# Six PSUM banks in place of two for the blocks of the FFN's input projection

## What is computed

```
def conv_ffn(h, w_in, conv_w, conv_b, w_out):
    u = dwconv_centred(jnp.einsum('bsd,df->bsf', h, w_in), conv_w, conv_b)
    gate, up = jnp.split(u, 2, axis=-1)
    return jnp.einsum('bsf,fd->bsd', jax.nn.gelu(gate, approximate=True) * up, w_out)
```

## Time and profile before

| what | before |
|---|---|
| median of three runs | 1570.83 us (1568.6 to 1573.79) |
| the profiled execution | 1573.15 us, span 1571.3 us |
| TensorE matmul busy | 1429.5 us, 91% |
| VectorE busy | 781.9 us, 50% |
| GpSimd busy | 690.0 us, 44% |
| ScalarE busy | 638.2 us, 41% |
| granted TensorE clock, mean | 0.952 of full |

### The profile page before, as it was taken

One profiled execution on the slowest core, in us unless ns is written; L12 is line 12 of the kernel. 1 busy time (PEld: TensorE's weight loads), 2 busy tenths in 40 slices (PEclk: granted clock), 3 DMA queues, 4 the chain that ended last, 5 costly groups with the idle time before them and its releaser, 6 DMA issues.

```text
span 1571.3 us, 15335 instructions
## 1 busy us (share of the span) xinstructions
PE 1429.5 (91%) x6054; PEld 1107.1 (70%) x6054; DVE 781.9 (50%) x936; ACT 638.2 (41%) x934; POOL 690.0 (44%) x339
## 2 busy tenths in 40 slices
PE   6899798989969999999997699987959999999994
PEld 4678565777846777777886477876737777778883
DVE  5435596661046766676001645355066676673004
ACT  5443474543334344434222455534334434443221
POOL 5343584023553444434554443422653444435543
PEclk9999899999988999999999699998969999999998
DMA  4222000012312332232332132310212332223331
GB/s 175 76 82 90 24 1 17 31 41 67 94 54 67 94 92 86 92 94 87 99 88 88 51 87 87 92 43 1 81 41 81 94 94 91 86 93 90 94 98 53
DMA packets 34631, 117.67 MB, mean 75 GB/s; under 512 B 3840, under 2 KB 4224, under 8 KB 34560
## 3 DMA queue, kind: packets, MB, share of 16 engines
q1 hardware_dynamic: 33840, 114.63, 23.5%
q10 hardware_dynamic: 720, 2.06, 0.4%
HBM read 114.58 MB, written 2.10 MB: 74 GB/s over the span
## 4 chain that ended last, share of the span: by engine, by line
PE 44%; DVE 29%; ACT 12%; issue 3%; DMA 0%; DVEq 0%; ACTq 0%
PE bank L254 12%; PE bank L257 12%; PE bank L258 12%; DVE cbuf L458 10%; ACT cbuf L502 4%; DVE cbuf L462 4%; ACT whi L230 3%; DVE ubuf L467 2%; DVE cbuf L532 2%; DVE cbuf L364 2%; DVE xw_lo L354 2%; ACT g_hi L511 2%; ACT cbuf L508 2%; PE bank L986 2%; DVE xres L374 1%
## 5 line engine op out<-in xcount | busy, mean ns | idle before, releaser
L238 POOL TENSOR_TENSOR wlo<-raw,whi 128x1024 fp32r<-128x1024 f32 (+2 forms) x217 | 505.3, 2331 | 752.1 <-ACT whi L230 752.1
L254 PE MATMUL bank<-xw_hi,whi 128*128 128x512 f32 x1224 | 509.1, 416 | 76.7 <-DVE xw_lo L354 62.9
L257 PE MATMUL bank<-xw_lo,whi 128*128 128x512 f32 x1224 | 492.2, 402 | 0.0
L258 PE MATMUL bank<-xw_hi,wlo 128*128 128x512 f32 x1224 | 492.1, 402 | 0.0
L254 PEld LDWEIGHTS bank<-xw_hi,whi 128*128 128x128 f32 x1224 | 234.7, 192 | 170.9 <-issue 54.6
L230 ACT ACTIVATE whi<-raw 128x1024 fp32r<-128x1024 f32 (+2 forms) x217 | 221.0, 1022 | 248.2 <-DMA raw<-in_fout 131.9
L258 PEld LDWEIGHTS bank<-xw_hi,wlo 128*128 128x128 f32 x1224 | 235.0, 192 | 57.3
L257 PEld LDWEIGHTS bank<-xw_lo,whi 128*128 128x128 f32 x1224 | 235.8, 193 | 56.0 <-issue 3.9
L458 DVE SCALAR_TENSOR_TENSOR cbuf<-ubuf,par,cbuf 128x510 f32<-128x510 f32 x100 | 183.4, 1834 | 126.5 <-ACT cbuf L502 115.9
L347 DVE RECIPROCAL rstd<-ubuf 128x512 f32<-128x512 f32 x4 | 13.4, 3353 | 363.8 <-ACT ubuf L324 363.8
L254 PE MATMUL bank<-g_hi,whi 128*128 128x512 f32 x352 | 139.4, 396 | 0.0
(11 more groups left out here) (240 smaller groups left out, 1486.0 us busy)
## 6 DMA issues: line engine op xcount, KB each, us to landing
raw<-in_fin SPq DMA_DIRECT2D x88, 512.0 KB, 3.5
raw<-in_fout SPq DMA_DIRECT2D x32, 448.0 KB, 3.2
raw<-in_gin SPq DMA_DIRECT2D x25, 512.0 KB, 3.6
raw<-in_hin SPq DMA_DIRECT2D x24, 512.0 KB, 3.5
raw<-in_hout SPq DMA_DIRECT2D x16, 512.0 KB, 3.5
raw<-in_fout SPq DMA_DIRECT2D x16, 512.0 KB, 3.5
raw<-in_gout SPq DMA_DIRECT2D x8, 512.0 KB, 3.5
xres<-in_x SPq DMA_DIRECT2D x8, 256.0 KB, 6.3
```

Of the source, the lines that this page charges most:

```text
L238: nc.gpsimd.tensor_tensor(wlo[s][:, 0:n], raw[s][:, 0:n], whi[s][:, 0:n].bitcast(F32), ALU.subtract).then_inc(w_lo, 1)
L254: first = nc.tensor.matmul(out_ap, wh, ah, start=start and k == 0, stop=False)
L257: nc.tensor.matmul(out_ap, wh, al, start=False, stop=False)
L258: last = nc.tensor.matmul(out_ap, wl, ah, start=False, stop=stop and k == kts - 1)
```

## The change

```diff
@@ -280,6 +280,8 @@
                     c = 2 * t + u
                     if c >= 2:
                         pe.wait_ge(sem("out_m"), of("out_m", k) + c - 1)
+                    elif k in (1, 3):
+                        pe.wait_ge(sem("fin_u"), of("fin_u", k // 2) + 2 * FF - 1 + c)
                     for b in range(per):
                         src_hi, src_lo, k0, ready = a_of_block(b)
                         if ready is not None and c == 0:
@@ -470,7 +472,7 @@
 
 
         def fbank(ft, u):
-            return bank[u if ft == 0 else 2 + u]
+            return bank[(2 * ft + u) % 6]
 
         def pe_fin(pe, l):
             base = BASE[f"fin{l}"]
@@ -478,8 +480,8 @@
 
             def body(t, ft):
                 for u in range(2):
-                    if ft >= 2:
-                        pe.wait_ge(sem("fin_u"), of("fin_u", l) + 2 * t - 1 + u)
+                    if ft >= 3:
+                        pe.wait_ge(sem("fin_u"), of("fin_u", l) + 2 * t - 5 + u)
                     if ft == 0 and u == 1:
                         product_and_res(pe, r, base + 1, fbank(ft, u)[:])
                     else:
```

## The result

The changed kernel takes 1573.85 us (median of 20 runs, 1571.25 to 1577.66) against 1571.16 us before (20 runs, 1568.01 to 1574.78). The ratio of the runs is 1.0021, with a 95% interval of 1.0011 to 1.0030, that is 1.7 to 4.7 us (the medians by themselves differ by 2.7 us). The interval leaves out 1.0, so the changed kernel is slower, by an amount that is small beside the spread of 6 us between its own runs.

A forecast was written before the change was run, and what follows sets the result against it. Fin was taken as bound by a ring of VectorE and ScalarE, 11.57 us a turn. Late fout starts (0.56 us) plus half clock (3.2) gave 3.8 us more, median 1570.83 to 1574.6 us, range 1570 to 1578.5.

The forecast's parts named there:

- No gain in fin: In fin, removing bank waits gains 0 on the path, since VectorE and ScalarE keep their 11.57 us turn.
- The next hold: In fin from block 17 on, TensorE waits for `w_lo` in place of the bank, about 14 times a layer.
- The late first matmul: At the handover, fout's first matmul starts 0.35 us late, net 0.28 us a layer, 0.56 in all.
- The ring's change: In fin, the ring of VectorE and ScalarE does not move and keeps its 11.57 us a turn.
- The clock: At the handover, TensorE's 3.75 us pause drops the clock, costing 1.6 us a layer, 3.2 in all, ends 0 and 4.4.
- Rival A: In fin, the bank holds the path, so the change gains 17.6 us in all: 1553.2 us; chance 0.05.
- Rival B: At the handover, no clock fall in one or both pauses, or shorter pause: 0.6 to 2.2 us lost; chance 0.20.
- rival C: Behind the handover pauses, half clock lasts 4.5 us or more each: for example 1575.8 or 1577.5 us; chance 0.25.
- Rival D: Inside fin, the clock falls too, at the pause each turn on `w_lo`: 33 us, 1604 us; chance 0.02.

The follow-up runs named there:

- e4: Kernel before (two banks), with ScalarE making the weights' high part of block j+3 behind the centre tap of block j: ratio 0.9912 to before.
- e1: Changed kernel (six banks), but TensorE waits until block j-2 has been taken out, so it can't run ahead: ratio 0.9999 to before.
- e2: Changed kernel with eight extra matmuls, results never read, between fin's last block and fout's first wait in both layers: ratio 1.0009 to before.
- e6: Changed kernel, but block 43 waits until block 41 has been taken out, which splits the pause: ratio 1.0015 to before.
- e3: Kernel before with four banks for fin (2 to 5), fout's chunks in banks 0 and 1 as before: ratio 1.0011 to before.
- e5: Changed kernel (six banks), with ScalarE making the weights' high part of block j+3 behind the centre tap of block j: ratio 0.9901 to before.

## Why the prediction was right

The forecast was 3.8 us more; the stages show 4.15, the runs 3.3 (1.7 to 4.7). Its mechanism is confirmed step by step; of its sizes one term that it put at nothing was not nothing, and that the half clock lasted as chosen was in part luck.

- No gain in fin: right. The ring kept its turn of 11.57 to 11.58 us. e4 shows directly that it was the ring, not TensorE, that set the turn.
- The next hold is the weights' low part, from block 17 on: right in place (block 17 starts behind a pause at 568.68, which is 82.93 us after the first block is taken out; the prediction's own numbers give 501.70 + 6 x 11.57 = 571.12, which is 82.8 behind 488.36). The waits do not name it, they say "issue"; the timeline does.
- The late first matmul: 0.28 us a layer net was forecast, 0.25 of it as a later start (in fin) and 0.10 of restart less 0.07 given back (in fout). Both are right: from block 42's `ubuf` instruction to fout's first matmul it is 0.74 us in place of 0.48 or 0.49, and fout is 0.03 to 0.05 us longer where the clock stays up in it (e1, e2, e6).
- The ring's change was put at nothing, and here the sum was short. From the first block taken out to block 42 it is 242.11 and 242.21 us in place of 241.95 and 241.89, so 0.16 and 0.32 us more. The first taps of the gate blocks (u=0) take 0.25 and 0.20 us more over the 22 turns. With six banks but no running ahead (e1) the same stretch is 241.94 and 241.90 us; in e2, e3 and e6, which all run ahead, it is 242.09 to 242.20. So the ring is slightly sensitive to when TensorE and the loads work, contrary to the prediction. Why the taps grew was not tried.
- The clock: 1.6 us a layer was chosen, from the pause of 3.05 us rather than that of 4.45 us. It was 3.4 us at half clock in both layers, and e2 prices it at 1.56 and 1.54 us. That the choice by the nearer length came out is partly luck, since the length of the pause does not set it: the very pause of 4.45 us brought 6.8 us of half clock, part of it inside the pause, in six of the eight kernels' profiled executions and 3.4 us in the two others (e1 and e5), and the pause of 1.98 us in e6 brought 3.4 us as well.
- Rival A (a gain) is out by the chain and by e3. Rival B (the clock stays up) and rival C (4.5 us of half clock or more) did not happen in the profiled execution; in other executions either may have, and the runs' times do not show it. Rival D (the clock falls in fin) did not happen: the window of 500 to 700 us reads 1.00.

A reader of the runs alone would have little to go by: the spans of the two profiled executions differ by only 1.6 us, since the changed kernel's came to fin 2.6 us earlier (485.75 against 488.36). No instruction ahead of that point differs between the two, and over the eight profiled executions it lies anywhere from 483.03 to 488.36 us (the last section shows one reason).

## What to carry to other kernels

Before giving an engine more buffers, follow the chain through the repeated wait. If it closes on the other engines, the buffers only let this engine run ahead to the next shared limit, and the time that it used to lose in small pieces can come back as one long pause where the stages meet. For TensorE one long pause can cost more than many short ones, because the clock can fall behind it. Shorten the ring first (here one instruction moved behind another, 13.6 us); after that it mattered little here whether there were two banks or six.

## What the runs showed of the hardware

- A pause of 1.98 us in the dense stream of fin's matmuls was followed by the half level in both layers (e6); pauses of 0.37 us a turn and of 1.46 us were not, in either layer. After pauses of 1.98, 3.24 and 3.54 us the half level lasted 3.4 us each time.
- The same pause need not bring the same clock. Behind one of 1.83 us in the attention stage, before the change and after it (windows of the kernel before, then of the changed one):

```profile
330.00:334.00 4.00, 4.00 (x12) 0.57 0.00 0
```

```profile
330.00:334.00 4.00, 4.00 (x19) 1.00 0.00 0
```

The first is (1 - 0.57) x 8 = 3.4 us at the half level, the second none; only 12 matmul records against 19 lie in the same 4 us. Of the other six kernels e4 fell there too, the rest did not. It also happens behind a pause as short as the harmless one of rows 4: in e5 a pause of 1.46 us between small matmuls of the second layer's mixer (it ends at 1031.03 us) was followed by 3.4 us of half level, while in the kernel before and the changed one the same pause was not. Such places can account for part of the scatter of some 5 us between runs of one kernel; how much was not measured.
